# Routing tables of a top-2 mixture of experts: home places from ranks, spare places in a branch

## The chip, the cores and the metric

The kernel is one launch on 1 core of a Trainium2 chip. The metric is the time of one execution on the device in microseconds (us): the median of three timed runs. A profile is one more execution, recorded by the hardware profiler.

Names of engines: PE is TensorE (matmuls), PEld its weight loads, DVE is VectorE, ACT is ScalarE, POOL is GpSimd, SP is SyncE, which issues DMAs.

## The reference

One layer of a transformer-like network over 256 context tokens and 1024 latent tokens (1280 rows of 1024 floats), with shared weights: attention and a pooling mixer, then a mixture of experts. The change touches the last part only:

```
g_logits = xf @ w_rg                                   # 4 groups
g_sel    = argmax(g_logits);  p_sel = softmax(g_logits)[g_sel]
e_in     = (xf @ w_re).reshape(-1, 4, 4)[g_sel]        # 4 experts of the group
top_v, top_i = top_k(e_in, 2)
w_top    = softmax(top_v) * p_sel
gate     = sum of one_hot(4 * g_sel + top_i, 16) * w_top
hid      = silu(x @ w_g[e]) * (x @ w_u[e]) * gate[e]   # 16 experts, 1024 -> 256
y        = sum over e of hid @ w_d[e]                  # 256 -> 1024
```

Every token goes to two of 16 experts. The kernel computes an expert only for the tokens that chose it.

## The kernel before

Up to about 1274 us the kernel computes modulation, projections, attention, pooling and the output projection; there the normalised rows `h2` go to DRAM (`h2d`) and the router's logits are ready for all ten token tiles of 128 rows. Then comes the routing, then 16 experts, then the final norm.

**The routing** turns the choice into tables. Each expert has two *home* tiles of T = 108 places (HOME = 2, HOMES = 32 in all); tokens beyond 216 of an expert go to *spare* tiles (SPARE = 20), SLOTS = 52 in all. DVE finds the chosen group and the two experts with `first_max` (a maximum, a comparison, a tie break), builds the one-hots `chosen` (one for each of the two picks) and their sum `either`. PE multiplies `either` by a triangle of ones, which gives each token's rank in its expert (`RANKS`, L1635 and L1637), and by ones, which gives the counts (L1638). DVE makes from the counts the number of spare tiles of each expert (`fills`, `n_tiles`, `ends`, `starts`), adds up each token's place (L2237 to L2246), divides it by T into a tile (`posA`) and a row in it (`posB`), and writes two one-hots, `above` over the 52 tiles and `hotB` over the 108 rows. PE multiplies `hotB` by `hotT` (`above` times the token's number) and gets a table with the token of each row of each tile (L1643), and by `hotW` (`above` times the high and low part of the weight) for the weights (L1647). DVE copies the ids (L2263) and `x_row` for the first two tiles (L2265); then it makes the spare tiles' owners, the count of spare tiles `n_spare`, the rows for the store (`out_ids`) and the weights (`w_slot`).

**The experts.** POOL gathers 108 rows of `h2d` for each tile by an indirect DMA: expert 0's two tiles at L1386, the others at L1396, where the tile of expert e + 1 or e + 2 follows PE's turn of an earlier one. PE turns the rows (L1661, `turn`), ACT casts them to xT (L1897), DVE makes the low part (L2286). PE multiplies the gate and up weights (L1672 with the high part and L1676 with the low part, `gate_up`), ACT and DVE make the hidden values, PE the down product (L1693, `down`), ACT scales it by `w_slot` (L1931), and POOL adds it to `y_sum` by a DMA. Each weight is split into a high part (ACT, L1891, L1902, L1906) and a low one (DVE, L2290, L2294). SP loads the weights one or two experts ahead.

The order of the work is written out by hand, one list for each engine; semaphores are the only link. `own.step` makes an engine wait for its own last instruction. PE, DVE, ACT and SP take their lists strictly in the order written. `if_spare` reads `n_spare` on PE, ACT, DVE and POOL and enters a loop over the spare tiles only if it is above zero; none of the loop's instructions has a record in the trace.

## Time and profile before

| | us |
|---|---|
| median of three timed runs | 1659.3 (1657.57 to 1660.28) |
| the profiled execution, whole | 1655.22 |
| its span in the trace | 1653.4 |
| PE busy in the span | 1542.7 |
| DVE busy | 981.2 |
| ACT busy | 645.2 |
| POOL busy | 293.2 |

Times within the trace are counted from the span's start. The mean granted clock of PE over the span is 0.966 of full; the profile's page shows it for 40 equal slices, and in the slice that holds the routing (1281 to 1323 us) it is 0.5. DMA is the mean busy share of the core's 16 DMA engines. In the rows further down, each row of a timeline has its start, its duration, the engine, the line, the operation and what it writes and reads; "x8" is a run of eight merged, and brackets hold the idle time before it and what ended that.

### The profile page before, as it was taken

What the parts mean: (1) busy time and instruction counts of PE and PEld (TensorE: products, weight loads), DVE (VectorE), ACT (ScalarE), POOL (GpSimd) and SP (SyncE); (2) the same over time, 40 slices, a digit from 0 to 9 for tenths busy, and PEclk for the clock granted to TensorE, in tenths of its full rate; (3) what the DMA queues carried; (4) which work ended last, traced back from release to release, by engine and by line L of the source; (5) the groups of instructions that cost most, each with busy time, mean ns of one, the idle gap of its engine ahead of it and who ended that gap; (6) DMA issues with size and microseconds to landing.
All of it is one profiled execution on the core that took longest, in us unless ns stands there. A gap on an engine that the chain in (4) does not pass through costs nothing.

```text
span 1653.4 us, 22244 instructions
## 1 busy us (share of the span) xinstructions
PE 1542.7 (93%) x8277; PEld 1284.7 (78%) x8277; DVE 981.2 (59%) x1457; ACT 645.2 (39%) x874; POOL 293.2 (18%) x229
## 2 busy tenths in 40 slices
PE   4899999999998889999999999999997599999975
PEld 3688888788887668887888887887886488888852
DVE  6488533045544377778777754334455677677727
ACT  6122121221113465666556621112222166766723
POOL 1021111123224100001000000000000134555420
PEclk9899999999999999999999999999998599999997
DMA  9135344220001010003000034326003369999965
GB/s 381 72 129 209 141 171 152 115 83 25 25 29 61 14 61 1 0 0 140 30 0 0 33 131 170 112 74 226 39 39 140 116 203 281 270 268 274 239 150 221
DMA packets 52731, 199.44 MB, mean 121 GB/s; under 512 B 8506, under 2 KB 17578, under 8 KB 41280
## 3 DMA queue, kind: packets, MB, share of 16 engines
q1 hardware_dynamic: 42432, 173.36, 28.9%
q0 software_dynamic: 10240, 25.28, 7.6%
q8 instruction: 39, 0.64, 0.2%
q14 instruction: 20, 0.16, 0.0%
HBM read 157.03 MB, written 44.63 MB: 122 GB/s over the span
## 4 chain that ended last, share of the span: by engine, by line
PE 42%; DVE 8%; DMA 6%; ACT 4%; issue 3%; POOL 1%; SPq 1%; DVEq 0%; POOLq 0%; ACTq 0%
PE psum L1542 8%; PE psum L1672 4%; PE psum L1498 4%; PE psum L1612 4%; PE psum L1693 3%; DMA xg<-h2d,x_row 3%; PE psum L1676 2%; PE psum L1621 2%; PE psum L1484 2%; PE psum L1481 2%; PE psum L1482 2%; PE psum L1467 2%; PE psum L1469 2%; PE psum L1468 2%; ACT prob L1769 2%
## 5 line engine op out<-in xcount | busy, mean ns | idle before, releaser
L351 PE MATMUL psum<-h_hi,w_hi 128*128 128x512 f32 (+1 forms) x768 | 198.3, 367 | 9.1 <-DVE h_lo L772 5.5
L351 PE MATMUL psum<-h_lo,w_hi 128*128 128x512 f32 (+1 forms) x768 | 193.9, 361 | 0.0
L351 PE MATMUL psum<-h_hi,w_lo 128*128 128x512 f32 (+1 forms) x768 | 192.9, 360 | 0.0
L2007 DVE TENSOR_TENSOR pT_lo<-psum,pT_hi 128x512 fp32r<-128x512 f32 x192 | 126.3, 686 | 55.2 <-ACT pT_hi L1775 55.0
L351 PEld LDWEIGHTS psum<-h_hi,w_hi 128*128 128x128 f32 x768 | 129.7, 191 | 33.3 <-issue 10.6
L351 PEld LDWEIGHTS psum<-h_lo,w_hi 128*128 128x128 f32 x768 | 129.3, 190 | 23.1
L351 PEld LDWEIGHTS psum<-h_hi,w_lo 128*128 128x128 f32 x768 | 128.8, 190 | 23.1
L669 POOL TENSOR_TENSOR w_lo<-w_raw,w_hi 128x1024 fp32r<-128x1024 f32 x32 | 79.7, 2493 | 358.6 <-ACT w_hi L525 358.6
L1775 ACT CAST pT_hi<-psum 128x512 fp32r<-128x512 f32 x192 | 104.5, 588 | 84.2 <-PE psum L1498 84.0
L810 DVE SCALAR_TENSOR_TENSOR ada_junk<-adaT,cs_rows 128x1024 f32<-128x1024 f32 x64 | 84.6, 1322 | 66.5 <-DMA adaT<-in_w_adaT 63.3
L1769 ACT ACTIVATE prob<-psum,nmax,q_row 128x1536 f32<-128x1536 f32 x64 | 104.6, 1634 | 32.5 <-DVE nmax L2001 32.5
L1498 PEld LDWEIGHTS psum<-ident,prob 128*128 128x128 f32 x768 | 91.0, 141 | 31.5 <-DVE pT_lo L2007 15.5
L1498 PE MATMUL psum<-ident,prob 128*128 128x128 f32 x768 | 112.0, 275 | 3.2 <-DVE pT_lo L2007 2.8
L1672 PE MATMUL psum<-xT,gu_hi 128*128 128x432 f32 x512 | 111.4, 371 | 2.2 <-DVE xT L2286 2.2
L1672 PEld LDWEIGHTS psum<-xT,gu_hi 128*128 128x128 f32 x512 | 97.0, 194 | 6.7 <-issue 2.5
L1481 PE MATMUL psum<-pT_hi,v_hi 128*128 128x512 f32 x192 | 88.7, 462 | 0.0
L1467 PE MATMUL psum<-kT_hi,q_hi 128*128 128x512 f32 x192 | 78.4, 408 | 6.9 <-DVE q_lo L2072 3.5
L2290 DVE TENSOR_TENSOR gu_lo<-gu_raw,gu_hi 128x2048 fp32r<-128x2048 f32 x32 | 73.3, 2294 | 19.3 <-ACT gu_hi L1902 19.1
L1469 PE MATMUL psum<-kT_hi,q_lo 128*128 128x512 f32 x192 | 76.6, 399 | 0.0
L1484 PE MATMUL psum<-pT_lo,v_hi 128*128 128x512 f32 x192 | 76.0, 396 | 0.1
L1468 PE MATMUL psum<-kT_lo,q_hi 128*128 128x512 f32 x192 | 75.8, 395 | 0.0
L1482 PE MATMUL psum<-pT_hi,v_lo 128*128 128x512 f32 x192 | 75.3, 392 | 0.0
(359 smaller groups left out, 2896.6 us busy)
## 6 DMA issues: line engine op xcount, KB each, us to landing
gu_raw<-in_w_gu SPq DMA_DIRECT2D x32, 1024.0 KB, 5.8
w_raw<-in_w_in SPq DMA_DIRECT2D x16, 1024.0 KB, 4.8
adaT<-in_w_adaT SPq DMA_DIRECT2D x16, 1024.0 KB, 6.1
dn_raw<-in_w_dn SPq DMA_DIRECT2D x16, 1024.0 KB
gates<-gst SPq DMA_DIRECT2D x14, 640.0 KB, 3.1
y_sum<-stage SPq DMA_DIRECT2D x12, 512.0 KB, 5.0
xt<-in_x SPq DMA_DIRECT2D x10, 512.0 KB, 6.9
merged<-gates SPq DMA_DIRECT2D x8, 640.0 KB, 3.9
```

Source lines behind the costliest of these rows:

```text
L351: mm = pe.matmul(psum[:, par_sets[j] + g:par_sets[j] + g + w], a[j][:, k, :], b[:, k, g:g + w], start=(k == 0 and a is w_hi and b is h_hi) ...
L1467: pe.matmul(o, q_hi[x.par][:, g, :], kT_hi[:, x.kv, k], start=True, stop=False)
L1468: pe.matmul(o, q_hi[x.par][:, g, :], kT_lo[:, x.kv, k], start=False, stop=False)
L1469: pe.matmul(o, q_lo[x.par][:, g, :], kT_hi[:, x.kv, k], start=False, stop=True).then_inc(s["a_scored"], 1)
L1481: pe.matmul(o, v_hi[v], pT_hi[b][g % 2][:], start=(c == 0), stop=False)
L1482: pe.matmul(o, v_lo[v], pT_hi[b][g % 2][:], start=False, stop=False)
L1484: mm = pe.matmul(o, v_hi[v], pT_lo[b][g % 2][:], start=False, stop=last)
L1498: mm = pe.transpose(psum[:, o:o + P], prob[x.par][:, h, k:k + P], ident[:])
L1542: mm = pe.matmul(psum[:, o + g:o + g + w], a[:, k, :], b[:, k, g:g + w], start=(k == 0 and a is w_h and b is a_hi), stop=(k == depth - 1 a ...
L1672: pe.matmul(psum[:, GU_PS[c][h]:GU_PS[c][h] + 4 * T], gu_hi[q][:, c, k, h * P:(h + 1) * P], xT[q][:, k, :], start=(k == 0), stop=False)
L1769: nc.scalar.activation(prob[x.par][:, g, 0:x.keys], psum[:, scores_at(x, g):scores_at(x, g) + x.keys], ACT.Exp, bias=nmax[:, x.par, g:g + ...
L2007: nc.vector.tensor_tensor(pT_lo[b][g % 2][:], psum[:, TP + 512 * b:TP + 512 * b + 512], pT_hi[b][g % 2][:], ALU.subtract).then_inc(s[f"a_t ...
```

## The change

Seven edits, all in the routing and what it feeds:

- DVE takes a token's place straight from its rank. `full` is 1 where the rank is 108 or more, `row` is the rank less 108 there; the tile's one-hot is `chosen` split by `full` into two halves (expert and half), so `hotT` and `above` have 32 columns in place of 52 and need neither the counts nor a division. `rest` takes one operation; `either` is made before `chosen`, from `picks`.
- PE signals when the ranks are done, before the counts' matmul.
- The softmax weights are worked out behind the second `hotB`, and `x_row` comes straight from the ids in PSUM; `hotW` is made behind it.
- PE's 20 weight matmuls become two groups of ten (`slot_weights`): one in front of the first turn, one behind the second.
- The counts' table (`slot_table`) goes behind expert 0's xT; the semaphore `r_rows` counts what is ready (1 and 2: x_row, 3: home ids and counts, 4: the table and home weights, 5: spare tables). POOL waits for 3 before it gathers expert 1, PE's `gate_up` of expert 0 for 3 and 4, and SP for 4 in place of the first xT low part before it loads the first two down weights.
- ACT casts expert 0's gate and up weights before the two exponentials, not behind them.
- The spare tiles' places, ids and weights are made in the branch that `if_spare` guards: some 45 operations on DVE, 40 matmuls and a reload of `route` there.

```diff
@@ sync
-                sp.wait_ge(s["e_x_lo"], 1)
+                sp.wait_ge(s["r_rows"], 4)
                 for q in range(2):
                     sp.dma_start(dn_raw[q][:], ...)
@@ gpsimd
                 pool.wait_ge(s["a_fill"], 16 * (TILES + 2))
+                pool.wait_ge(s["r_rows"], 3)
                 load_x(1, 0)
@@ tensor
+                mm.then_inc(s["r_ranks"], 1)
                 pe.matmul(psum[:, COUNTS:COUNTS + n], ones_r[:], m, start=True, stop=True).then_inc(s["r_ranks"], 1)
...
-                pe.wait_ge(s["r_onehot"], 3)
-                for c in range(2 * TILES):
-                    mm = pe.matmul(psum[0:T, WEIGHTS:WEIGHTS + 2 * SLOTS], hotB[:, c, :], hotW[:, c, :, :].rearrange("p n s -> p (n s)"),
-                                   start=(c == 0), stop=(c == 2 * TILES - 1))
-                mm.then_inc(s["r_weights_ps"], 1)
+                def slot_weights(first):
+                    pe.wait_ge(s["r_onehot"], 3)
+                    for c in range(first, first + TILES):
+                        mm = pe.matmul(psum[0:T, WEIGHTS:WEIGHTS + 2 * HOMES], hotB[:, c, :], hotW[:, c, :, :].rearrange("p n s -> p (n s)"),
+                                       start=(c == 0), stop=(c == 2 * TILES - 1))
+                    if first:
+                        mm.then_inc(s["r_weights_ps"], 1)
...
+                slot_weights(0)
                 turn(0, 0)
                 turn(0, 1)
+                slot_weights(TILES)
                 over_experts(pe, step)
@@ vector
-                own.step(ts(rest[:], pick[0][:], -1.0, 1.0, ALU.mult, ALU.add))
-                own.step(tt(rest[:], rest[:], e_in[:], ALU.mult))
-                own.step(ts(e_in[:], pick[0][:], -3.0e38, None, ALU.mult))
-                own.step(tt(rest[:], rest[:], e_in[:], ALU.add))
+                own.step(nc.vector.scalar_tensor_tensor(rest[:], pick[0][:], -3.0e38, e_in[:], ALU.mult, ALU.add))
                 first_max(pick[1], eeq, rest[:], v2[:])
+                own.step(tt(picks[:], pick[0][:], pick[1][:], ALU.add))
+                own.step(tt(either[:].rearrange("p t (e g) -> p t g e", g=EG), gsel[:].unsqueeze(3).broadcast_to(g44), picks[:].unsqueeze(2).broadcast_to(g44), ALU.mult))
+                dve.sem_inc(s["r_mask"], 1)
                 own.step(tt(v2[:], v2[:], v1[:], ALU.subtract))
...
+                dve.wait_ge(s["r_ranks"], 1)
+                own.step(ts(full[:], rank, float(T), None, ALU.is_ge))
+                own.step(nc.vector.scalar_tensor_tensor(row[:], full[:], -float(T), rank, ALU.mult, ALU.add))
+                for c in range(2):
+                    own.step(tt(by_pick[:, c], row[:], chosen[:, c], ALU.mult))
+                own.step(nc.vector.reduce_sum(pos[:], by_pick[:], AX.X))
...
+                for c in range(2):
+                    own.step(tt(halves(hot)[:, c, :, 1, :], chosen_tok[:, c], full[:], ALU.mult))
+                    own.step(tt(halves(hot)[:, c, :, 0, :], chosen_tok[:, c], halves(hot)[:, c, :, 1, :], ALU.subtract))
+                    tt(hotB[:, c * TILES:(c + 1) * TILES, :], flat[...], col, ALU.is_equal).then_inc(s["r_onehot"], 1)
...
+                dve.wait_ge(s["r_ids_ps"], 1)
+                for j in range(2):
+                    ts(x_row[j][0:T, :], psum[0:T, IDS + j:IDS + j + 1], -1.0, 0.0, ALU.add, ALU.max).then_inc(s["r_rows"], 1)
...
                 gu_low(0, 0, 0)
-                gu_low(0, 0, 1)
                 x_low(0, 0, 0)
                 x_low(0, 0, 1)
+                slot_table()
+                gu_low(0, 0, 1)
                 over_experts(dve, step)
```

How this moves instructions on VectorE, from the ranks to the second one-hot of the rows. Before (from the places' sum on; ahead of these rows stand seven operations on the counts, and `count` itself):

```order
L2239 TENSOR_SCALAR beyond<-psum 128x160
L2240 TENSOR_TENSOR beyond<-beyond,starts 128x160
L2241 TENSOR_TENSOR place<-psum,route 128x160
L2242 TENSOR_TENSOR place<-place,beyond 128x160
...
L2253 SCALAR_TENSOR_TENSOR posB<-posA,pos 128x20
L2254 TENSOR_TENSOR above<-posA,route 128x1040
L2257 TENSOR_TENSOR hotT<-above,route 128x520
L2259 TENSOR_TENSOR hotB<-posB,route 128x1080
L2257 TENSOR_TENSOR hotT<-above,route 128x520
L2259 TENSOR_TENSOR hotB<-posB,route 128x1080
```

The same stretch after the change, whole:

```order
L2251 TENSOR_SCALAR full<-psum 128x160
L2252 SCALAR_TENSOR_TENSOR row<-full,psum 128x160
L2254 TENSOR_TENSOR by_pick<-row,chosen 128x160 x2
L2255 TENSOR_REDUCE pos<-by_pick 128x20
L2261 TENSOR_TENSOR hotT<-chosen_tok,full 128x160
L2262 TENSOR_TENSOR hotT<-chosen_tok,hotT 128x160
L2263 TENSOR_TENSOR hotB<-pos,route 128x1080
L2261 TENSOR_TENSOR hotT<-chosen_tok,full 128x160
L2262 TENSOR_TENSOR hotT<-chosen_tok,hotT 128x160
L2263 TENSOR_TENSOR hotB<-pos,route 128x1080
```

From the first operation on the ranks or counts to the second `hotB` DVE has 25 instructions before and 11 after; those on the counts are no longer among them.

On TensorE, from the weight matmuls to expert 0's first products. Before:

```order
L1647 MATMUL psum<-hotW,hotB 108x104 [waits x_in2]
L1647 MATMUL psum<-hotW,hotB 108x104 x19
L1661 MATMUL psum<-ident,xg_3191 128x108 [waits x_in8]
L1661 MATMUL psum<-ident,xg_3191 128x108 x7
L1661 MATMUL psum<-ident,xg_3192 128x108 [waits x_in9]
L1661 MATMUL psum<-ident,xg_3192 128x108 x7
```

After, where `xg` with the lower number is expert 0's first tile:

```order
L1661 MATMUL psum<-hotW,hotB 108x64 [waits x_in2]
L1661 MATMUL psum<-hotW,hotB 108x64 x9
L1676 MATMUL psum<-ident,xg_3198 128x108 [waits x_in8]
L1676 MATMUL psum<-ident,xg_3198 128x108 x7
L1676 MATMUL psum<-ident,xg_3199 128x108 [waits x_in9]
L1676 MATMUL psum<-ident,xg_3199 128x108 x7
L1661 MATMUL psum<-hotW,hotB 108x64 [waits x_in2]
L1661 MATMUL psum<-hotW,hotB 108x64 x9
```

Ten weight matmuls stay in front of the turns and ten now stand between them and the products.

## Rows read from the trace of the kernel before

**Rows 1.** Stretches by granted clock: the experts, PE busy, clock, DMA share, GB/s.
```profile
1345.00:1585.00 240.00, 237.73 (x1448) 1.00 0.93 257
```

**Rows 2.** Timeline of PE, from the ranks to the end of the experts.
```profile
1282.29 2.00 PE L1637 MATMUL psum<-either,ones_r 128*128 128x144 f32 x9
...
1294.47 3.93 PE L1643 MATMUL psum<-hotT,hotB 128*108 128x52 f32 x20 [9.84 <-DVE hotB L2259]
1298.83 3.84 PE L1647 MATMUL psum<-hotW,hotB 128*108 128x104 f32 x20 [0.43 <-DVE hotW L2261]
1305.30 1.70 PE L1661 MATMUL psum<-ident,xg 108*128 108x108 f32 x8 [2.63 <-DMA xg<-h2d,x_row]
1307.35 1.70 PE L1661 MATMUL psum<-ident,xg 108*128 108x108 f32 x8 [0.35 <-DMA xg<-h2d,x_row]
1311.21 4.74 PE L1672 MATMUL psum<-xT,gu_hi 128*128 128x432 f32 x16 [2.15 <-DVE xT L2286]
1315.78 1.94 PE L1676 MATMUL psum<-xT,gu_lo 128*128 128x216 f32 x16
1319.61 0.96 PE L1661 MATMUL psum<-ident,xg 108*128 108x108 f32 x8 [1.89 <-DMA xg<-h2d,x_row]
1321.82 1.70 PE L1661 MATMUL psum<-ident,xg 108*128 108x108 f32 x8 [1.24 <-DMA xg<-h2d,x_row]
1323.20 5.49 PE L1672 MATMUL psum<-xT,gu_hi 128*128 128x432 f32 x16
...
1336.05 1.15 PE L1693 MATMUL psum<-dn_hi,hid_hi 128*108 128x512 f32 x4
...
1344.55 1.09 PE L1693 MATMUL psum<-dn_hi,hid_hi 128*108 128x512 f32 x4
...
1598.52 9.98 PE L1744 MATMUL psum<-x,ident 128*128 128x512 f32 x16 [5.43 <-ACT yst L1931]
```

**Rows 3.** Timeline of DVE, the routing and two later places.
```profile
1280.61 0.92 DVE L2211 TENSOR_TENSOR chosen<-gsel,pick 128x160 f32<-128x160 f32 x2 [0.15 <-DVE v L2208]
1281.56 0.33 DVE L2212 TENSOR_TENSOR either<-chosen,chosen 128x160 fp32r<-128x160 f32 x1
...
1284.73 0.33 DVE L2227 TENSOR_REDUCE count<-psum 128x16 f32<-128x160 f32 x1 [0.97 <-PE psum L1638]
...
1295.06 1.28 DVE L2259 TENSOR_TENSOR hotB<-posB,route 128x1080 fp32r<-128x1080 f32 x1
...
1298.69 0.20 DVE L2263 TENSOR_SCALAR ids<-psum 108x52 int32<-108x52 f32 x1
1298.93 0.21 DVE L2265 COPY x_row<-ids 108x1 int32<-108x1 int32 x2
...
1299.58 0.49 DVE L2269 TENSOR_REDUCE owner<-past 128x20 f32<-128x320 f32 x1
...
1333.66 2.29 DVE L2294 TENSOR_TENSOR dn_lo<-dn_raw,dn_hi 128x2048 fp32r<-128x2048 f32 x1
...
1610.93 2.44 DVE L2353 TENSOR_TENSOR y<-y,gt_row 128x1024 f32<-128x1024 f32 x2 [24.72 <-DMA y<-y_sum]
```

**Rows 4.** Timeline of DMA issues: the first gather, down weights, expert 1's second gather.
```profile
1300.17 1.20 POOL L1386 DMA_INDIRECT xg<-h2d,x_row  x1 [393.57 <-issue]
...
1309.12 0.81 SPq L1337 DMA_DIRECT2D dn_raw<-in_w_dn  x2
1310.96 1.08 POOL L1396 DMA_INDIRECT xg<-h2d,x_row  x1 [0.93 <-POOL x_row L1394]
```

**Rows 5.** Stretches of 1 us: busy PE, PEld, DVE, ACT, POOL, then clock, DMA.
```profile
1314.00:1315.00 1.00, 1.00 (x7) 0.96 (x6) 0.09 (x1) 0.00 (x0) 0.00 (x0) 0.92 1.13 356
...
1321.00:1322.00 1.00, 0.18 (x1) 0.19 (x2) 0.48 (x1) 0.49 (x1) 0.15 (x1) 0.50 0.87 328
...
1327.00:1328.00 1.00, 1.00 (x5) 0.93 (x4) 0.38 (x1) 1.00 (x2) 0.00 (x0) 0.60 0.26 66
```

**Rows 6.** Timeline of ACT: expert 1's second cast of turned rows.
```profile
1323.55 0.88 ACT L1897 CAST xT<-psum 128x864 fp32r<-128x864 f32 x1 [2.07 <-PE psum L1661]
```

More of the change, by code:

```diff
@@ L1080, in build @@
         by_expert = routed("by_expert", [P, TILES, EG, EPG])
-        chosen = [routed(f"chosen{c}", [P, TILES, EPG, EG]) for c in range(2)]
+        picks = routed("picks", [P, TILES, EPG])
+        chosen_tok = routed("chosen_tok", [P, 2, TILES, NE])
+        by_pick = routed("by_pick", [P, 2, TILES, NE])
+        full, row = (routed(n, [P, TILES, NE]) for n in ("full", "row"))
         either = routed("either", [P, TILES, NE], F32R)
-        place = routed("place", [P, TILES, NE])
         rsum = routed("rsum", [P, TILES])
@@ L1087, in build @@
         fills = routed("fills", [P, NE, FILLS])
-        n_tiles, ends, starts = (routed(n, [P, NE]) for n in ("n_tiles", "ends", "starts"))
+        starts = routed("starts", [P, NE])
         sums = routed("sums", [P, NE, NE])
@@ L1115, in build @@
         w_top = kept("w_top", [P, 2, TILES], F32)
+        chosen = kept("chosen", [P, 2, TILES, NE], F32)
+        ranks = kept("ranks", [P, TILES, NE], F32)
+        n_tiles, ends = (kept(n, [P, NE], F32) for n in ("n_tiles", "ends"))
         assert k_at[0] <= RHL + 60 * KB
@@ L1121, in build @@
             o += w
-        for n in "g_max e_sum e_dif e_w mask ranks onehot ids_ps weights_ps x_row dve_c".split():
+        for n in "g_max e_sum e_dif e_w mask ranks onehot ids_ps weights_ps rows dve_c".split():
             s["r_" + n] = sem("b4_" + n)
@@ L2260, in _ @@
-                own.step(tt(hotW[:, :, 0, :], above[:], w_hi_top[:].unsqueeze(2).broadcast_to(ab), ALU.mult))
-                tt(hotW[:, :, 1, :], above[:], w_lo_top[:].unsqueeze(2).broadcast_to(ab), ALU.mult).then_inc(s["r_onehot"], 1)
-                dve.wait_ge(s["r_ids_ps"], 1)
-                own.step(ts(ids[0:T, :], psum[0:T, IDS:IDS + SLOTS], -1.0, 0.0, ALU.add, ALU.max))
-                for j in range(2):
-                    nc.vector.tensor_copy(x_row[j][0:T, :], ids[0:T, j:j + 1]).then_inc(s["r_x_row"], 1)
@@ new lines, in _ @@
+                split_weights()
+                for c in range(2):
+                    own.step(tt(halves(above[:])[:, c, :, 1, :], chosen[:, c], full[:], ALU.mult))
+                    own.step(tt(halves(above[:])[:, c, :, 0, :], chosen[:, c], halves(above[:])[:, c, :, 1, :], ALU.subtract))
+                ab = [P, 2 * TILES, HOMES]
+                above_ = above[:].rearrange("p c t n -> p (c t) n")
+                own.step(tt(hotW[:, :, 0, :], above_, w_hi_top[:].unsqueeze(2).broadcast_to(ab), ALU.mult))
@@ new lines, in _ @@
+                tt(hotW[:, :, 1, :], above_, w_lo_top[:].unsqueeze(2).broadcast_to(ab), ALU.mult).then_inc(s["r_onehot"], 1)
+                own.step(ts(ids[0:T, 0:HOMES], psum[0:T, IDS:IDS + HOMES], -1.0, 0.0, ALU.add, ALU.max))
+                own.step(nc.vector.tensor_copy(ranks[:], rank))
+                dve.wait_ge(s["r_ranks"], 2)
+                count_ps = psum[:, COUNTS:COUNTS + TILES * NE].rearrange("p (t e) -> p e t", e=NE)
+                own.step(nc.vector.reduce_sum(count[:], count_ps, AX.X))
```

172 lines of the change are left out of this document (107 added, 65 removed).

## The prediction

> **What bounds the kernel now.** I read the granted clock and busy shares by stretch first, then the timelines of TensorE (PE) and VectorE (DVE) around the routing, then the DMA issues. From 1345 to 1585 us PE is busy 237.7 of 240 us at the full clock while the DMA engines are 0.93 busy [rows 1]: the experts are paced by PE, and their work is the same after the change. What comes before is not paced by PE: from 1284.29, when the rank matmuls end, to 1311.21, when the first expert's products begin, PE runs 20 small matmuls for ids, 20 for weights and two turns of 8, and stands otherwise [rows 2]. DVE holds it up: it works from the wake-up at 1284.73 without a real pause to the ids' copy at 1298.93 [rows 3]. Everything behind waits for that copy, which releases the gathers; so a microsecond taken from this chain should be one of the run, if what follows keeps up.
>
> **Up to the mask.** Before, the mask `either` ends at 1281.56 + 0.33 = 1281.89 [rows 3]. In front of it: of the four small operations that make `rest` (0.20 each, as the ids' copy [rows 3], with the 0.03 that stands between dependent ones) one is left: -0.69. The difference v2 - v1 with its semaphore step (0.33) and the two `chosen` products (0.92 + 0.03) go behind: -1.28. `either` was 0.36 and becomes a small sum, 0.23, and one product that writes as `chosen` does, 0.47 with its pause: +0.34. Sum -1.63: mask at 1280.26. The rank matmuls end 2.40 after it (1282.29 + 2.00 less 1281.89) [rows 2], and DVE no longer waits for the counts matmul: it reads at 1280.26 + 2.40 + 0.10 = 1282.76. The moved operations and two new `chosen_tok` products (0.14 + 0.33 + 0.95 + 0.72 = 2.1) lie in that wait, with 0.4 to spare.
>
> **From the ranks to the ids.** Before: count at 1284.73, second `hotB` ends 1295.06 + 1.28 = 1296.34: 11.61 us. After: full 0.35, row 0.36, two products 0.72, one reduction over 320 elements 0.49 + 0.03, four `hotT` operations of 160 elements, two `hotB` of 1.28. The four write every second float, which no row of before shows. Contiguous 160 elements cost 0.33 (`either`), `chosen`, which writes every fourth float, 0.46 each [rows 3]. That bounds them: 4 x 0.36 = 1.44 or 4 x 0.49 = 1.96. Sum 1.95 + 2.56 + (1.44 to 1.96) = 5.95 to 6.5, so from 1282.76 the second `hotB` ends at 1288.7 to 1289.2.
> The Trainium skill (SBUF — State Buffer, section Door 1: The DMA port swizzle) says that SBUF is read and written in lines of 16 bytes and that a stride is free as long as two accesses fall in a line. By it `chosen` pays for its stride of 16 bytes, which the 0.46 beside 0.33 bears out, and the 8-byte writes here would be free: the low end. I don't lean on it and take the middle.
> From the second `hotB` to the ids took 2.35 (1296.34 to 1298.69: ten matmuls of 0.196, they are as long with 52 columns as the weights' with 104 [rows 2], so 32 columns save nothing). The ids' copy for all slots (0.24, from 1298.69 to 1298.93) is no longer in front of x_row. x_row starts at 1291.1 to 1291.6 in place of 1298.93: **7.3 to 7.8 us earlier, I take 7.6**. The six softmax operations (1.35) lie in the wait for the ids, which is 2.35.
>
> **From x_row to the first products.** Call x_row's time X. Before: turns at X + 6.37 and X + 8.42, products at X + 12.28 [rows 2, 3]. PE takes its work in order, and two groups of ten weight matmuls now stand in front of the first turn and of the first products. First group: behind x_row DVE does the split (0.42), four `above` (1.44 to 1.96), two `hotW` of 640 elements (0.49 at 320 and 1.28 at 1080 elements [rows 3] give 0.82, so 1.7): ready at X + 3.8 to 4.3, done by PE 0.1 + 1.92 later, at X + 5.8 to 6.3. The gather lands at X + 6.37: hidden, but with 0.07 to 0.6 us to spare. Second group: X + 10.1 to X + 12.0, before xT is ready at X + 12.28: hidden by 0.2. If the cover were gone each would cost what it sticks out. The count table, 2.4 us on DVE, stands behind xT and before the second gu_lo, which PE needs only at X + 24: hidden. ScalarE's (ACT) two casts of 1.9 us move from behind the exponentials to a time when it idled: hidden, nothing gained.
> So the first products start at 1311.21 - 7.6 = 1303.6.
>
> **Expert 1's rows.** Here is a second gain. Before, PE finished expert 0's first products at 1315.78 + 1.94 = 1317.72, then waited until 1319.61 and 1321.82 for the two gathers of expert 1. The second was issued at 1310.96, beside 2 MB of down weights issued at 1309.12, and took 10.9 us; expert 0's first gather, alone, took 5.13 (1300.17 to 1305.30) [rows 2, 4]. After the change SyncE waits for the count table, X + 14.6 = 1305.9, to load the down weights, while expert 1's second gather goes at X + 12.0 as before, and the first ahead of it. Alone, the second lands at X + 17.2. PE asks for it at X + 12.3 + (6.5 to 7.9) + 0.8 = X + 19.6 to 21.0. The 6.5 is before's duration; the clock rose to full (2.4 from 1.2 GHz) 2.9 us after these products began (0.92 in the stretch 1314 to 1315 [rows 5]); how much of them runs at the low clock may shift from run to run: expert 0's second 16, low for all but their last microsecond, took 5.49 [rows 2, 5], and with such 16 and a part of the next 16 low the whole is 7.9. So the wait goes.
> The next bound is a chain of ACT and DVE. Let T be the end of expert 1's second xT cast (1323.55 + 0.88 = 1324.43 [rows 6]). After it come the table load, sigmoid, a gu_hi cast, the dn_hi cast, expert 0's second hidden part and dn_lo, which ends at 1333.66 + 2.29 = 1335.95 [rows 3]; PE begins the down products at 1336.05 [rows 2], T + 11.6. This chain is left as it is. PE alone would be there at T + 9.5 at the full clock, so a new wait of some 2 us for dn_lo stands at this place, and the gain is T's. T was X + 25.5; it becomes X + 12.28 + (6.5 to 7.9) + 2.5 = X + 21.3 to 22.7. Gain: 7.6 + 2.8 to 4.2 = 10.4 to 11.8. The traced run had its clock fall at 1321 [rows 5] between the two turns, which made T 0.8 later than in a run without this; a usual run has some of that less. **I take 10.8.**
>
> **The rest.** Expert 2's gathers are released by expert 1's turns; the first goes at some X + 20.8 = 1312.1 and, even at 10.9, lands at 1323.0, while PE stands for dn_lo until 1324 to 1325. From the down products on PE's order is the same and nothing gives back. Behind the experts the untaken branch is longer: DVE has 24.7 us idle there, PE waits 5.4 for ACT [rows 2, 3]; POOL's grows by one DMA and two waits. Costed at nothing.
> Profile: 1655.22 (span 1653.4) - 10.8 = 1644.4. The three timed runs have a median of 1659.3, 4.1 above the profiled one; by the same gain **1648.5**.
>
> **The rivals.**
> 1. The gathers of expert 1 stay slow. If the second still takes 10.9, it lands at X + 22.9 and T is X + 24.7: gain 7.6 + 0.8 = 8.4, 1650.9. For it: the down weights start 2.6 us behind the second gather. Against: the lone gather needs 5.1 in all, so only its tail is met.
> 2. The chain gives less: DVE's strided operations cost over 0.49, so that both one-hots and the first weight group are late, and PE's order passes it on. At 0.25 more for each of eight, 2 us: with rival 1's loss the gain is 6.4, 1652.9.
> 3. The stage is paced by DMA and gives the gain back. Its share is 0.93 [rows 1], and the first load behind the routing moves only from 1309.12 to 1305.9. Then the gain is 3.2: 1656.1, at the edge of what a measurement tells (0.2%, 3.3 us). Against: PE idles but 2.3 us in 240, a queue that paces would show more.
> 4. Slower than before: the clock. The new 2 us wait at expert 0's down products lets the clock fall, as it did at 1321 when PE had done one turn of eight since 1317.72 [rows 2, 5], and waits that recur each half expert keep it low. A half expert is 8.5 us at the full clock (1336.05 to 1344.55 [rows 2]) and some 15.6 at the low one (an estimate: 16 products with 432 columns in 5.8, 16 with 216 in 3.1, 12 with 512 in 5.1, a turn of 1.7; the full clock's durations nearly doubled). Two such eat 14.2 us: 1662.7 (+3.4). It decides beyond 30 us at the low clock. Against: it rose 2.9 and 4.6 us after product work began at both places, and one fall costs 2 to 3 us only.
> 5. The skipped branch stalls. The Trainium skill (Runtime: NRT & Kernel Launch, Instruction fetch mechanics) says that a taken branch whose target has not been fetched waits for the fetch. Before's jump over a shorter body shows none beyond PE's 5.4 us wait for ACT. As a mechanism of this kernel: PE jumps over 40 more matmuls and their weight loads, and is needed again at 1612 for 5 us of joins, so over 9 us of stall is needed before it costs anything; at two loaded transfers, 22 us, it is -10.8 + 13 = +2: 1661.5.
>
> **How the numbers follow.** Forecast 0.62 (1648.5, its own range 1646 to 1651). Rival 1 0.18, rival 2 0.08, rival 3 0.07, rival 4 0.04, rival 5 0.01. The range for 8 in 10 takes in rivals 1 and 2 and, below, a gain of 11.8 with runs as low as 1657.6: 1645 to 1655. Faster by over 0.2%: forecast, rivals 1, 2: 0.88. Within: rival 3 and a little of 4: 0.08. Slower: 0.04.
>
> **What would show it.** Steps right: the first ids matmul at about 1287 in place of 1294.47; x_row some 7.6 us earlier; `hotT` at 0.33 to 0.46; the first turn 6.4 us behind x_row and the first products 12.3; no wait for xg at expert 1; a wait for dn_lo at the first down products near 1325; from there to the end the same distance as before. Wrong: a turn that begins right behind a weight matmul (group one on the path); gathers of 10 us; half experts of over 9 us; a DMA share near 1 with waits for xg of microseconds.

## The result, and the profile after

| | before | after |
|---|---|---|
| median of 8 runs each, on one chip (us) | 1658.43 (1652.73 to 1662.14) | 1646.72 (1641.94 to 1653.46) |
| ratio after / before, 95% interval | | 0.9937 [0.9921, 0.9953] |
| the profiled execution, whole | 1655.22 | 1649.31 |
| its span | 1653.4 | 1647.5 |
| DVE busy | 981.2 | 974.2 |
| PE busy | 1542.7 | 1544.4 |

The forecast was 1648.5; the change brings 0.63%, 10.4 us by the ratio (7.8 to 13.1). The two profiled executions differ by 5.9 us only. That is no contradiction: the stages that the change does not touch end at 1273.72 in the one and at 1280.75 in the other (the start of the router's logits on DVE), and over all traces shown here that point lies between 1273.7 and 1287.3. So every distance below is counted from the logits of its own trace, or from X, the start of x_row. One execution of a_gu_ahead_again took 3899.37 us and is left out of its median in the table further down.

TensorE after, the same stretch as [rows 2]:

```profile
1287.72 2.00 PE L1648 MATMUL psum<-either,ones_r 128*128 128x144 f32 x9
...
1293.85 3.89 PE L1655 MATMUL psum<-hotT,hotB 128*108 128x32 f32 x20 [3.79 <-DVE hotB L2263]
1301.59 2.01 PE L1661 MATMUL psum<-hotW,hotB 128*108 128x64 f32 x10 [3.85 <-DVE hotW L2288]
1304.52 1.70 PE L1676 MATMUL psum<-ident,xg 108*128 108x108 f32 x8 [0.92 <-DMA xg<-h2d,x_row]
1306.38 1.70 PE L1676 MATMUL psum<-ident,xg 108*128 108x108 f32 x8 [0.15 <-DMA xg<-h2d,x_row]
1307.76 1.99 PE L1661 MATMUL psum<-hotW,hotB 128*108 128x64 f32 x10
1310.34 5.20 PE L1691 MATMUL psum<-xT,gu_hi 128*128 128x432 f32 x16 [0.59 <-DVE xT L2316]
1315.38 1.94 PE L1695 MATMUL psum<-xT,gu_lo 128*128 128x216 f32 x16
1317.16 1.65 PE L1676 MATMUL psum<-ident,xg 108*128 108x108 f32 x16
...
1331.57 2.01 PE L1712 MATMUL psum<-dn_hi,hid_hi 128*108 128x512 f32 x4 [2.17 <-DVE dn_lo L2324]
1333.38 1.75 PE L1712 MATMUL psum<-dn_lo,hid_hi 128*108 128x512 f32 x4
...
1341.56 1.09 PE L1712 MATMUL psum<-dn_hi,hid_hi 128*108 128x512 f32 x4
```

Expert 1's second xT cast, whose end the prediction calls T, and expert 0's `dn_lo`:

```profile
1318.10 1.66 ACT L1926 CAST xT<-psum 128x864 fp32r<-128x864 f32 x2 [0.22 <-PE psum L1676]
1329.18 2.28 DVE L2324 TENSOR_TENSOR dn_lo<-dn_raw,dn_hi 128x2048 fp32r<-128x2048 f32 x1
```

The wait ahead of the ids is 3.79 in place of 9.84. Both turns of expert 1 are now one run of 16 right behind expert 0's products: the waits of 1.89 and 1.24 for `xg` are gone. In their place stands the wait of 2.17 for `dn_lo`. A half expert is the stretch from one group of down products to the next, two for each expert. The first (from 1331.57 to 1341.56) takes 9.99 against 8.50 before, because the matmuls at its head are slow. The stretches of 1 us show the clock there, to be read as [rows 5]:

```profile
1331.00:1332.00 1.00, 0.43 (x1) 0.44 (x2) 1.00 (x2) 1.00 (x1) 0.51 (x1) 0.70 1.01 410
1332.00:1333.00 1.00, 1.00 (x4) 0.64 (x3) 1.00 (x2) 0.53 (x2) 0.56 (x1) 0.50 0.89 377
...
1335.00:1336.00 1.00, 1.00 (x7) 0.72 (x6) 0.87 (x3) 0.38 (x1) 0.58 (x1) 1.00 0.00 0
```

From full it falls to 0.50, the level of 1.2 GHz, behind a stretch in which PE did one turn of eight and waited, and it is back at full by 1335.

VectorE after, to be held against [rows 3]:

```profile
1286.87 0.44 DVE L2235 TENSOR_TENSOR either<-gsel,picks 128x160 fp32r<-128x160 f32 x1
...
1287.78 0.93 DVE L2240 TENSOR_TENSOR chosen<-gsel,pick 128x160 f32<-128x160 f32 x2
...
1289.84 0.32 DVE L2251 TENSOR_SCALAR full<-psum 128x160 f32<-128x160 f32 x1 [0.41 <-PE psum L1648]
...
1294.07 0.33 DVE L2262 TENSOR_TENSOR hotT<-chosen_tok,hotT 128x160 fp32r<-128x160 f32 x1
1294.43 1.28 DVE L2263 TENSOR_TENSOR hotB<-pos,route 128x1080 fp32r<-128x1080 f32 x1
...
1297.85 0.23 DVE L2276 TENSOR_SCALAR x_row<-psum 108x1 int32<-108x1 f32 x2 [0.93 <-PE psum L1655]
```

From `full` to the end of the second `hotB` it is 1295.71 - 1289.84 = 5.87 us, where it was 11.61 from `count` on.

### The profile page after: what moved, and what is told of

Read it like the earlier page. It is cut to its first block, busy times and chain, and to the rows that moved or that the text cites. A ratio compares the mean times of both kernels' runs of the same rounds, so it can differ in the third digit from the quotient of the medians.

```text
span 1647.5 us, 22242 instructions
## 1 busy us (share of the span) xinstructions
PE 1544.4 (94%) x8277; PEld 1287.6 (78%) x8277; DVE 974.2 (59%) x1448; ACT 646.4 (39%) x874; POOL 302.0 (18%) x229
## 4 chain that ended last, share of the span: by engine, by line
PE 43%; DVE 8%; DMA 6%; ACT 4%; issue 2%; POOL 1%; SPq 1%; DVEq 0%; POOLq 0%; ACTq 0%
PE psum L1553 8%; PE psum L1691 4%; PE psum L1509 4%; PE psum L1623 4%; PE psum L1712 3%; DMA xg<-h2d,x_row 3%; PE psum L1695 2%; PE psum L1632 2%; PE psum L1495 2%; PE psum L1492 2%; PE psum L1493 2%; PE psum L1478 2%; PE psum L1480 2%; PE psum L1479 2%; ACT prob L1798 2%
## 5 line engine op out<-in xcount | busy, mean ns | idle before, releaser
L1410 POOL DMA_INDIRECT y_sum<-yst,y_row x32 | 74.6, 2330 | 28.3 <-POOL y_row L1408 28.3
```

## The experiments

All traces in one table: us from the logits to the start of x_row, and to the start of the down products (with `dn_hi` and `hid_hi`) of the first, the second and the 31st of the 32 half experts; then the median of each, the median of the kernel before on the same chip, and the ratio. The medians are a coarser measure than the distances: they carry the spread ahead of the logits. The distances have a limit too: each row is one trace, and the changed kernel's three differ by 2.2 us at the 31st.

| kernel | x_row | 1st | 2nd | 31st | median | before | ratio [95%] |
|---|---|---|---|---|---|---|---|
| before | 25.21 | 62.33 | 70.83 | 313.64 | | | |
| b_mask_first | 23.93 | 61.33 | 69.84 | 312.56 | 1653.03 | 1658.29 | 0.9971 [0.9953, 0.9989] |
| b_dn_late | 25.19 | 59.02 | 68.96 | 313.18 | 1653.76 | 1658.29 | 0.9971 [0.9951, 0.9990] |
| after | 17.10 | 50.82 | 60.81 | 303.31 | 1646.72 | 1658.43 | 0.9937 [0.9921, 0.9953] |
| after_again | 17.12 | 51.44 | 61.53 | 305.02 | 1648.55 | 1656.83 | 0.9943 [0.9923, 0.9963] |
| after_third | 17.10 | 51.54 | 61.62 | 305.48 | 1647.87 | 1657.49 | 0.9931 [0.9908, 0.9953] |
| a_counts_front | 19.52 | 53.65 | 63.73 | 306.62 | 1650.13 | 1656.83 | 0.9966 [0.9947, 0.9985] |
| a_weights_front | 17.10 | 51.08 | 61.07 | 303.32 | 1644.65 | 1656.83 | 0.9929 [0.9908, 0.9951] |
| a_dn_early | 17.09 | 52.90 | 61.43 | 304.99 | 1649.31 | 1658.29 | 0.9932 [0.9908, 0.9955] |
| a_dn_first | 17.10 | 49.07 | 61.05 | 306.25 | 1646.77 | 1658.29 | 0.9917 [0.9895, 0.9940] |
| a_gu_ahead | 17.11 | 49.23 | 57.73 | 302.39 | 1644.73 | 1656.83 | 0.9922 [0.9903, 0.9940] |
| a_gu_ahead_again | 17.10 | 49.21 | 57.74 | 301.44 | 1644.11 | 1657.49 | 0.9924 [0.9900, 0.9947] |
| a_gather_soon | 17.10 | 51.00 | 61.06 | 300.27 | 1641.82 | 1657.49 | 0.9908 [0.9887, 0.9929] |
| a_both | 17.11 | 48.54 | 57.05 | 296.96 | 1640.91 | 1657.49 | 0.9892 [0.9871, 0.9914] |

**b_mask_first: the mask alone, on the kernel before.**

```diff
-                own.step(ts(rest[:], pick[0][:], -1.0, 1.0, ALU.mult, ALU.add))
...
+                own.step(nc.vector.scalar_tensor_tensor(rest[:], pick[0][:], -3.0e38, e_in[:], ALU.mult, ALU.add))
+                own.step(tt(eeq[:], pick[0][:], pick[1][:], ALU.add))
+                own.step(tt(either[:]..., gsel[:]..., eeq[:]..., ALU.mult))
+                dve.sem_inc(s["r_mask"], 1)
                 own.step(tt(v2[:], v2[:], v1[:], ALU.subtract))
...
-                own.step(tt(either[:], chosen[0][:]..., chosen[1][:]..., ALU.add))
-                dve.sem_inc(s["r_mask"], 1)
```

> The kernel before with the edits up to the mask alone: one operation for rest, either made ahead of chosen from the sum of the picks. My theory: the first rank matmul comes 1.6 us earlier behind the logits, and since DVE's chain behind it is bound by the ranks, x_row, the products and the end all come 1.6 us (less up to 0.7 if DVE, which has the moved work and the softmax in that wait, is then the late one) earlier: 0.9 to 1.6. Rival (the chain is not what sets the end): PE's rank matmuls move, the first products or the end do not.

x_row starts 1.28 us earlier (25.21 to 23.93), the first down products 1.00, the 31st 1.08. In the changed kernel the mask ends 6.56 from the logits against 8.17 before, so the mask's own term is 1.61 (predicted 1.63). Alone it brings 0.3 less, because here DVE has `chosen` and the softmax weights to make in the wait for the counts and gets to `count` without any wait left, 0.45 us behind the end of the counts' matmul. The mask is 1.3 of the 8.1 us at x_row; the rest is the shorter chain behind the ranks. The ratio gives more than the distances, 4.8 us (1.8 to 7.8), and its interval doesn't reach down to the 1.1 us of the trace; the difference isn't explained.

**a_counts_front: the counts back in front, on the changed kernel.**

```diff
+                dve.wait_ge(s["r_ranks"], 2)
+                own.step(nc.vector.reduce_sum(count[:], count_ps, AX.X))
...
+                own.step(nc.vector.reduce_sum(ends[:], sums[:], AX.X))
                 own.step(ts(full[:], rank, float(T), None, ALU.is_ge))
...
-                own.step(nc.vector.reduce_sum(count[:], count_ps, AX.X))
...
-                    own.step(nc.vector.reduce_sum(ends[:], sums[:], AX.X))
```

> The changed kernel with the wait for the counts' matmul and the five operations on the counts back in front of full, as they stood before the change. They take 0.33 + 0.35 + 0.35 + 0.42 + 0.42 us with pauses of 0.03 to 0.04 and, first, some 0.4 us more for the counts. Theory (DVE's chain from ranks to ids is the path, term by term): x_row starts 2.3 to 2.5 us later counted from the logits (19.5 in place of 17.1), and the end moves by the same. From X on nothing changes except that the down loads may go up to 1.9 us earlier with respect to X, beside expert 1's second gather: a wait for it of under 1 us. Rival (the gathers or loads pace the stage): x_row moves but the down products and the end stay within 0.5 us.

DVE of this kernel:

```profile
1285.45 0.33 DVE L2253 TENSOR_REDUCE count<-psum 128x16 f32<-128x160 f32 x1 [0.78 <-PE psum L1650]
1285.81 0.36 DVE L2254 TENSOR_TENSOR fills<-count,route 128x192 f32<-128x192 f32 x1
...
1287.04 0.42 DVE L2258 TENSOR_REDUCE ends<-sums 128x16 f32<-128x256 f32 x1
1287.50 0.32 DVE L2259 TENSOR_SCALAR full<-psum 128x160 f32<-128x160 f32 x1
```

x_row stands at 19.52, 2.41 later, and the first down products 2.1 to 2.8, the 31st 1.1 to 3.3 later than in the three traces of the changed kernel (2.0 against their mean of 304.60). That is the theory's 2.3 to 2.5 at x_row, and it reaches the down products. At the 31st it agrees in the mean, but the spread between traces is as large as the effect, and the ratio's interval overlaps that of after_again. The rival, a stage that does not care when it starts, wanted the down products within 0.5 us, and falls there. Both turns of expert 1 still follow without a wait.

**b_dn_late: the loads behind the gathers, on the kernel before.**

```diff
-                sp.wait_ge(s["e_x_lo"], 1)
+                sp.wait_ge(s["e_x_lo"], 2)
+                sp.wait_ge(s["e_gu"], 1)
                 for q in range(2):
                     sp.dma_start(dn_raw[q][:], ...)
```

> The kernel before with one edit: SP loads the first two down weights (2 MB) only behind expert 0's first products (1317.7 in place of 1309.1). It tests the second half of the gain alone. My theory: expert 1's two gathers then travel alone and take about 5 us in place of 10.9, PE's waits for xg at expert 1 (1.9 and 1.2 us) go, and the end of expert 1's second xT cast comes 2.8 to 4.2 us earlier behind x_row; the down weights land some 3 us later than they did, with a gate and up load beside them, so ACT's dn_hi cast may wait 1 to 2 us and give part of that back: 1.5 to 4 us faster. Rival (the gathers are slow for a reason of their own, or the stage is paced by DMA): the gathers still take about 10 us, PE waits as before, no gain.

With the loads issued at 1320.71, behind the first half of expert 0's gate and up products, PE runs as follows:

```profile
1320.44 1.65 PE L1662 MATMUL psum<-ident,xg 108*128 108x108 f32 x16
...
1334.10 1.19 PE L1662 MATMUL psum<-ident,xg 108*128 108x108 f32 x8 [2.16 <-DMA xg<-h2d,x_row]
```

Expert 1's waits are gone as in the changed kernel. Its two gathers landed 4.7 and 5.6 us after their issue; T is X + 21.90 (X + 25.50 before), and the first down products stand 3.31 earlier although x_row did not move. So the second gain is separate from the first. But the loads now meet expert 2's gather: PE waits 2.16 us for it, the clock falls to 0.50 behind that wait, and the second down products are only 1.87 earlier, the 31st 0.46. Where the loads go decides which gather pays. Here too the ratio gives more than the trace: 4.8 us (1.7 to 8.1), for 1.5 to 4 expected.

**a_dn_early: the loads ahead again, on the changed kernel.**

```diff
-                sp.wait_ge(s["r_rows"], 4)
-                for q in range(2):
+                sp.wait_ge(s["e_x_lo"], 1)
+                for q in (1, 0):
+                    if q == 0:
+                        sp.wait_ge(s["r_weights_ps"], 1)
+                        sp.wait_ge(s["e_gu_lo"], 1)
```

> The changed kernel, but SP loads the down weights earlier: dn_raw of expert 1 at the first xT low part, as the kernel before did, dn_raw of expert 0 behind the last weight matmul and the first gu_lo (2.4 us earlier than in the changed kernel). So the loads are issued beside expert 1's second gather and not 2.6 us behind it. My theory: that gather takes 8 to 11 us again in place of some 5, so PE waits 1 to 3 us for xg at expert 1's second turn, and the end is up to 3 us later. Rival (the wait went because everything before it moved, not because of the loads' place): no wait for xg, same time as the changed kernel.

Loads issued from 1310.04 on, gather of expert 1's second tile at 1311.67: expert 1's gathers landed 8.1 and 10.7 us after their issue (4.8 and 5.3 in the changed kernel, where the loads were issued at 1312.46), and PE again stands before expert 1's second turn.

```profile
1320.08 0.91 PE L1679 MATMUL psum<-ident,xg 108*128 108x108 f32 x8
1322.44 0.96 PE L1679 MATMUL psum<-ident,xg 108*128 108x108 f32 x8 [1.45 <-DMA xg<-h2d,x_row]
```

T is X + 24.18 in place of X + 21.9 to 22.6, and the first down products are 1.4 to 2.1 later. That is rival 1's mechanism, seen when it is provoked, and it is what the change avoids. By the second down products the loss is gone (61.43 against 60.81 to 61.62): here the clock stayed full behind a wait of 1.95, and the half expert took 8.53. So the loss doesn't reach the end, where up to 3 us were expected. The stretch behind that wait, and below it the same one of a_weights_front (the next experiment), where the wait was 1.96 and the clock fell:

```profile
1336.00:1337.00 1.00, 1.00 (x5) 0.74 (x6) 1.00 (x2) 1.00 (x2) 0.19 (x1) 1.00 1.00 426
```

```profile
1328.00:1329.00 1.00, 1.00 (x4) 0.64 (x3) 1.00 (x1) 0.00 (x0) 1.00 (x1) 0.50 0.20 82
```

**a_weights_front: both groups of weight matmuls ahead of the turns.**

```diff
                 slot_weights(0)
+                slot_weights(TILES)
                 turn(0, 0)
                 turn(0, 1)
-                slot_weights(TILES)
```

> The changed kernel with both groups of ten weight matmuls in front of the first turn, in place of one group ahead of it and one behind the second turn. Theory (the second group was hidden between the turns and the products): PE is busy with both until X + 7.8, so the first turn starts 1.1 us later than the gather allows, at X + 7.8 in place of 6.7; the second turn begins by X + 9.5, 1.0 later; the first products at X + 13.5 in place of 12.5, and all that follows, the end too, 1.0 us later. Rival (the second group already costs its own time where it stands, between the second turn and the products): the first turn is later but the products begin at the same time, and the end does not move.

```profile
1296.47 3.81 PE L1661 MATMUL psum<-hotW,hotB 128*108 128x64 f32 x20 [3.85 <-DVE hotW L2288]
1300.09 3.14 PE L1676 MATMUL psum<-ident,xg 108*128 108x108 f32 x16
1305.52 5.17 PE L1691 MATMUL psum<-xT,gu_hi 128*128 128x432 f32 x16 [2.29 <-DVE xT L2316]
```

Here the expectation missed. The first turn starts at X + 7.36, 0.7 to 1.0 later than in the changed kernel's traces, but the second needs no wait any more and ends with it: the second gather lands only 2 us behind the first and had bounded both. The products start at X + 12.79 against 12.49 to 12.69, and the end does not move (31st 303.32). So the split into two groups is worth 0.1 to 0.3 us at the first products, not 1.0, and nothing that can be seen at the end.

**a_dn_first: `dn_lo` ahead of expert 1's second `gu_lo`, and on ACT `dn_hi` ahead of its second `gu_hi`** (DVE's part of the edit; ACT's `gu_high` moves alike).

```diff
@@ vector
-                    if more(e, 1):
+                    if more(e, 1) and later(e, 1):
                         gu_low(e + 1, 1 - q, 1)
                     else:
                         dn_low(e, q)
                     hidden(e, 1)
                     hidden_low(e, q, 1)
+                    if not later(e, 1):
+                        gu_low(e + 1, 1 - q, 1)
...
```

> The changed kernel with a new order in expert 0's step alone: ACT casts dn_hi ahead of expert 1's second gu_hi (which goes behind expert 0's hidden parts), DVE makes dn_lo ahead of the second hidden part and gu_lo behind it. It takes away the wait of 2.2 us for dn_lo in front of the first down products, after which the changed kernel's clock fell for 2.7 us. My theory: the wait shrinks to under 0.5 us, the clock stays at full, and the next down products come 3 to 3.7 us earlier behind the second xT cast; the gu_lo that was moved back is needed 7 us later and hides: 2 to 3.7 us faster than the changed kernel. Rival (dn_lo is not what is late; hidden parts or PE are): the wait stays at about 2 us under another name, no gain.

The wait for `dn_lo` is gone: `dn_lo` ends at X + 29.57 and the first down products start at X + 31.97 straight behind a turn, 1.8 to 2.5 earlier. But the cast that was moved behind is late next, and with it `x_low` of expert 2:

```profile
1330.65 1.09 PE L1712 MATMUL psum<-dn_hi,hid_lo 128*108 128x512 f32 x4
1333.48 0.93 PE L1676 MATMUL psum<-ident,xg 108*128 108x108 f32 x8 [1.74 <-DVE xT L2318]
```

The clock fell behind this wait as it did behind the old one, and the half expert took 11.98. The second down products stand at 61.05, where they were, and the 31st at 306.25, 0.8 to 2.9 later: the expectation of 2 to 3.7 us missed. Work pushed back on an engine came back as a wait, 1.74 us in place of 2.2.

**a_gu_ahead: the same cast moved forward, into idle time.** In the changed kernel ACT idles 6.57 us until expert 0's first products are done and DVE 2.09 until expert 1's turned rows are cast, and expert 1's second gate and up weights can be split there. ACT's `gu_high` moves as DVE's `gu_low` does.

```diff
@@ vector
                     if not later(e, 1):
+                        gu_low(e + 1, 1 - q, 1)
                         x_low(1, 1, 0)
                         x_low(1, 1, 1)
...
-                    if more(e, 1):
+                    if more(e, 1) and later(e, 1):
                         gu_low(e + 1, 1 - q, 1)
                     else:
                         dn_low(e, q)
                     hidden(e, 1)
                     hidden_low(e, q, 1)
-                    if more(e, 1):
+                    if more(e, 1) and later(e, 1):
                         dn_low(e, q)
```

> The changed kernel with expert 1's second gu_hi cast (ACT, 1.9 us) and second gu_lo (DVE, 2.3 us) moved into time in which both engines idled before expert 1's turned rows arrive; expert 0's dn_hi and dn_lo follow 2 us and 4.5 us sooner. Theory (the down side's new wait is a chain of casts, and the clock falls in it): dn_lo ends near X + 29 in place of X + 33.6, PE has no wait for it, the down products start at X + 32.0 in place of 33.7, the clock stays full, the first half expert takes 8.5 us in place of 10.0; 3.2 us in all at the second down products and at the end. Nothing is displaced behind it, as it was when dn_lo was put in front of gu_lo. Rival (something else is late next, as then): the 1.7 us come back as a wait of the same size before the next turn, and the end moves by under 1 us.

> The moved casts alone once more. Theory and rival of the last group agree on the start: second down products at 57.7 from the logits in place of 60.8 to 61.5. What is open is the end, which moved by only 0.9 to 2.6 us in the one trace: if the giving back is regular, the last down products stand at 302 to 303 again and waits for gathered rows sum to some 3.3 us; if it was chance, at 300 to 301 and the waits to 1.4 to 2.8.

```profile
1335.65 0.90 PE L1676 MATMUL psum<-ident,xg 108*128 108x108 f32 x8
1336.56 1.14 PE L1712 MATMUL psum<-dn_hi,hid_hi 128*108 128x512 f32 x4
...
1345.06 1.09 PE L1712 MATMUL psum<-dn_hi,hid_hi 128*108 128x512 f32 x4
```

No wait, and 8.50 from the one to the other: the clock stays at full (1.00 in each stretch from 1334 to 1338). In both traces the second down products stand at 57.7, 3.1 to 3.9 earlier, as expected. Of this 0.9 to 4.0 is left at the 31st. Some 0.7 us goes regularly: the second half expert takes 9.07 to 9.09 in both, with a wait of 0.49 and 0.46 for `dn_lo`. The small waits for gathered rows sum to 3.3 and 2.5 us, where the changed kernel has 1.4, 2.8 and 2.9. The second trace lies between what was expected of a regular giving back (302 to 303, 3.3 us) and of chance (300 to 301), so it leaves that undecided. The question that this leaves is whether the stage is at the limit of its DMA, as rival 3 had it.

**a_gather_soon: an expert's first gather ahead of the addition to y_sum.**

```diff
                 def step(e, q):
                     if more(e, 2):
-                        load_x(e + 2, 0)
                         load_x(e + 2, 1)
                     if later(e, 1):
                         add_y(e - 1, 0)
+                    if more(e, 3):
+                        load_x(e + 3, 0)
+                    if later(e, 1):
                         add_y(e - 1, 1)
...
                 load_x(1, 1)
+                load_x(2, 0)
```

> The changed kernel as the reference of this group. All theories: as in the two traces so far, counted from the logits: x_row 17.1, first down products 50.8 to 51.4, second 60.8 to 61.5, last (of the 32 half experts, the 31st) 303.3 to 305.0, waits for gathered rows of 1.4 to 2.8 us in all between.

> The changed kernel once more, as the reference for three edits of it on one chip. X is x_row's start, counts are from the start of the logits' row. Theory: its milestones repeat within 0.2 us: x_row at 17.1, first turn X + 6.4 to 6.7, expert 1's second xT cast ends at X + 21.9, dn_lo ends at X + 33.6, the down products start at X + 33.7 after a wait of 2.2 us, and the first half expert takes 10.0 us because the clock falls in that wait. Rival: the fall was a feature of one execution, and the half expert takes 8.5 us here.

> The changed kernel with the gather of an expert's first tile put ahead of the preceding addition to y_sum on POOL, where it stood behind. In the traces so far that gather was issued 6.5 us after the turn that frees its buffer, took up to 10.9 us beside the weights and kept PE waiting 0.2 to 1.1 us every third to fifth expert. Theory (the stage is paced by PE, and its small waits come from POOL's order): the gather goes 3 to 4 us sooner, the waits for gathered rows go, and the way from the second down products to the last shrinks from 242.5 to 243.5 us to 240.5 to 241.5; the end 1.4 to 2.8 us sooner. Rival (the DMA engines pace it: 0.93 busy): the waits come back at the same size on weights, the additions or the other tile's gather, and nothing moves.

The two repeats give the spread of the changed kernel. x_row, the wait of 2.2 us and the slow half expert behind it (10.1 us in both) repeat, so the fall of the clock there was no feature of one execution; the 31st down products lie at 303.3, 305.0 and 305.5.

In the older order (POOL, of a_gu_ahead) the gather waits behind an addition, whose `yst` comes late; in the new one it goes as soon as PE's turn has freed the buffer. The turn that waited for its rows stands below it:

```profile
1487.18 0.98 POOL L1408 COPY y_row<-out_ids 108x1 int32 x1 [2.14 <-ACT yst L1960]
1489.04 1.61 POOL L1410 DMA_INDIRECT y_sum<-yst,y_row  x1 [0.88 <-POOL y_row L1408]
1490.09 1.88 POOL L1401 COPY x_row<-out_ids 108x1 int32 x1
1492.96 1.11 POOL L1403 DMA_INDIRECT xg<-h2d,x_row  x1 [0.99 <-POOL x_row L1401]
```

```profile
1503.86 0.96 PE L1676 MATMUL psum<-ident,xg 108*128 108x108 f32 x8 [1.12 <-DMA xg<-h2d,x_row]
```

The turn that frees the buffer began at 1485.65; the gather was issued at 1492.96, and its rows were there at 1503.86, 10.9 us later. With the gather put ahead it follows 2.3 us behind the start of its turn (1482.16) in place of 7.3; POOL reads:

```profile
1483.32 0.18 POOL L1403 COPY x_row<-out_ids 108x1 int32 x1 [0.76 <-PE psum L1681]
1484.48 1.09 POOL L1405 DMA_INDIRECT xg<-h2d,x_row  x1 [0.97 <-ACT yst L1965]
```

All waits of PE from the first down products on (us in all, times, longest; first group: changed kernel, 1330 to 1580; second: a_gather_soon, 1325 to 1575):

```profile
PE psum L1712 <- DVE dn_lo L2324: 2.2, 1, 2.2
PE psum L1676 <- DMA xg<-h2d,x_row: 1.4, 4, 0.6
```

```profile
PE psum L1717 <- DVE dn_lo L2329: 2.2, 1, 2.2
PE psum L1717 <- ACT yst L1965: 1.3, 1, 1.3
```

No wait for gathered rows is left. From the second to the 31st down products it is 239.21 us, against 242.50, 243.49 and 243.86 in the changed kernel, shorter by more than the 1.4 to 2.8 us expected. The waits that the view names were not all: a half expert without one takes 8.44 us, that with the wait of 0.40 took 9.06, and one with none on record 8.75. In a_gather_soon each of the 26 half experts behind the first takes 8.44 or 8.45. With the same work and loads, the stage is 3.3 to 4.6 us shorter, at a DMA share of 0.93 as before. So it was not the DMA engines' throughput that held it, but the place of one gather in POOL's order; its latency beside the weight loads, up to 10.9 us, made that place matter.

**a_both: the two together.**

> The earlier gather and expert 1's second gate and up casts moved ahead, together, on the changed kernel. Theory (the gain of the casts was given back only through waits for gathered rows): second down products at 57.7 from the logits, last at 298.5 to 299.5 in place of 303.3 to 305.0, so 4.5 to 5.5 us at the end. Rival (DMA paces the stage and gives back what the start gains): second down products at 57.7, but the last at 302 to 303, as with the casts alone.

```profile
PE psum L1717 <- ACT yst L1965: 1.3, 1, 1.3
PE psum L1717 <- DVE dn_lo L2331: 0.5, 1, 0.5
```

The second down products stand at 57.05, the 31st at 296.96, 6.4 to 8.5 earlier than in the changed kernel. That is more than the 4.5 to 5.5 expected, and 1.5 below the 298.5 that was the lower bound: the gather's part had been put too small, as in a_gather_soon. What a_gu_ahead gained at the first down products is kept here but for the 0.7 us of the second half expert. The median is 1640.91, 7.0 below the changed kernel's 1647.87 of the same group, and the ratio to the kernel before 0.9892. Between a_both and a_gather_soon the intervals overlap; the distances (296.96 and 300.27) tell them apart by 3.3 us, in one trace each.

## Why the prediction was right

Step by step, each against the changed kernel's three traces:

- **The mask**: predicted 1.63 earlier, measured 1.61 (8.17 to 6.56 from the logits). The 2.1 us of operations moved behind it were hidden, with 0.41 of wait left on DVE ahead of `full`; predicted was 0.4.
- **Ranks to ids**: predicted 5.95 to 6.5, taken at 6.2; measured 5.87. The four `hotT` operations cost 0.32 to 0.33 each, the low end, though I took the middle. The rule of the Trainium skill (SBUF — State Buffer, Door 1: The DMA port swizzle) that a stride is free while two accesses fall in one line of 16 bytes gave this end. The trace agrees: 160 elements at a stride of 8 bytes 0.33, as contiguous ones, at 16 bytes 0.44 (`either`) and 0.46 (`chosen`).
- **Second `hotB` to x_row**: predicted 2.35, measured 2.14 (before 2.59, with the copy of all ids in front). x_row is 8.11 us earlier; I took 7.6 of 7.3 to 7.8. The half microsecond more is 0.3 from `hotT` and 0.2 here.
- **First turn and products**: X + 6.38 to 6.67 and X + 12.49 to 12.69 for X + 6.37 and X + 12.28. The weight groups were hidden as said, but the reserve was larger than I gave it: a_weights_front shows that the second gather bounds the pair of turns.
- **Expert 1's rows**: no wait in any trace of the changed kernel; T at X + 21.91, 22.52 and 22.64, predicted 21.3 to 22.7. b_dn_late and a_dn_early show the cause from both sides: move the loads, and the wait goes or comes. What that is worth at the end they don't show (0.46 us at the 31st in the one, nothing from the second down products on in the other).
- **The new wait**: predicted about 2 us, measured 2.17 to 2.19, the down products at T + 11.8 (predicted 11.6). a_gu_ahead shows that it is the chain of casts: two of them moved, and it is gone.
- **The clock in that wait** was not in the forecast's sum. It cost the half expert 10.0 to 10.1 us in place of 8.5, in all three traces. This is rival 4's mechanism at one place; it did not recur, so its price was 1.5 us and not 14.2. It took back more than x_row had given above the forecast: first down products 10.8 to 11.5 us earlier, second 9.2 to 10.0, the 31st 8.2 to 10.3.
- **Behind the experts**: nothing like rival 5's 22 us. PE waits 4.51 there against 5.43 [rows 2], DVE 23.27 against 24.72 [rows 3]. A stall shorter than these waits could hide in them. (The skipped part has 35 operations on DVE, not some 45.)

```profile
1594.34 8.74 PE L1773 MATMUL psum<-x,ident 128*128 128x512 f32 x16 [4.51 <-ACTq L2004]
```

- **The way from the 31st to the end** was costed at nothing, and it varies: 66.04 us before, 63.44, 63.42 and 65.33 in the changed kernel, 64.27 and 64.46 in the two variants of the kernel before. The turns of the final norm, one group of 16 above, took 8.65 to 8.74 us in the two short ones and 9.94 in the third (before 9.98 [rows 2]); the granted clock is 0.50 at their start for some 4 us in the one case and 6 in the other. So from the logits to the end the changed kernel is 8.9 to 12.9 us shorter, and what goes beyond the 8.2 to 10.3 at the 31st is for the most part this clock, which differs between traces of one kernel.

Sum: 10.8 predicted; by the ratios of three groups 10.4, 9.4 and 11.4 us. The mechanism is the predicted one up to the first down products. That the sum agrees to 0.4 us is luck in part: x_row gave half a microsecond more, the clock took 1.5, and the first ratio's interval is 5 us wide. Of the rivals, 1 appears only when provoked (a_dn_early), 2 is out by 0.33 for each strided operation, 4 struck once only, and 3 is out by a_gather_soon, in which the same loads keep up with a stage 3.3 to 4.6 us shorter. The waits for `xg` in the experts' midst stay (1.7 us before; 1.4, 2.8 and 2.9 after). The prediction said that nothing gives back from the down products on, and that was not so: 10.8 to 11.5 at the first became 9.2 to 10.0 at the second, by the clock, and 8.2 to 10.3 at the 31st.

Open is why the clock stayed full in a_dn_early behind a wait of 1.95 us and fell in a_weights_front behind one of 1.96; in a_dn_early PE had also waited 1.45 us some 13 us before. Open too is why single traces of one kernel differ by 2.2 us at the 31st half expert, and why the ratios of b_mask_first and b_dn_late are larger than their distances. Of the kernel before there is one trace only, so its distances have no spread of their own.

## What to carry to other kernels

Find the chain that releases the first gather and take out of it all that the first tiles don't need: tables for the rest can follow behind the first transfers. When a wait goes, look for casts on other engines that are late next, and move them forward into idle time that exists; moved backward (a_dn_first) they came back as a wait elsewhere. An engine that issues DMAs in order can hold a gather behind a transfer whose data is late; a DMA share of 0.93 did not mean that DMA was the bound.

## What the runs showed of the hardware

- A wait of PE of 2.2 us with a turn of eight ahead of it cost more than itself: the granted clock fell to 0.50 behind it (1332 to 1334 in the changed kernel), and the half expert took 10.0 to 10.1 us for 8.5, in the three traces of the changed kernel and in a_counts_front and a_gather_soon. It fell likewise behind 1.96 us in a_weights_front and 1.74 us in a_dn_first, but not behind 1.95 us in a_dn_early: the length of the wait alone does not tell.
- An indirect gather of 108 rows of 4 KB landed 4.4 to 5.6 us after its issue with no weight load issued before it (expert 1's, in the changed kernel's three traces and b_dn_late), and PE waited up to 10.9 us from issue to rows where weight loads ran, at the start of the experts (before) and in their midst (a_gu_ahead).
- POOL's copy of 108 single values took 0.18 to 0.20 us in 27 of 28 rows behind a gather, but 0.97 to 2.36 in 26 of 31 behind an addition to `y_sum` (changed kernel, 1320 to 1600 us); what it waits for there no run tells.
